# Expert activations turned by VectorE, the last two experts as half ones, sums from DRAM added by GpSimd, and the final norm in a branch

## The chip, the cores and the metric

The kernel runs on one core of a Trainium2 chip. The metric is the device time of one launch in microseconds. PE is TensorE, PEld its weight loads, DVE is VectorE, ACT is ScalarE, POOL is GpSimd, SP is SyncE, which here only issues transfers. Tensors are fp32.

## What is computed

One decoder block on 512 tokens of 1024 features. The first part (a gated linear recurrence, a dilated attention and their projections) is not touched. The second part is a mixture of 32 experts, of which each token takes four:

```python
def _clamped_swiglu(u):
    glu = jnp.minimum(u[..., ::2], SWIGLU_LIMIT)
    lin = jnp.clip(u[..., 1::2], -SWIGLU_LIMIT, SWIGLU_LIMIT)
    return glu * jax.nn.sigmoid(SWIGLU_ALPHA * glu) * (lin + 1.0)
...
    u = xb @ w_up[e] + b_up[e]            # w_up[e] 1024 x 2048
    return _clamped_swiglu(u) @ w_down[e] + b_down[e]   # w_down[e] 1024 x 1024
...
    x = x + _moe(_rmsnorm(x, norm2_g[l]), ...)
return _rmsnorm(x, final_norm_g)
```

The weights of one expert are 8 MB (up) and 4 MB (down), all 32 are 403 MB, and each is read once.

## The kernel before

**Places.** The experts are done in 32 places, numbered p. DVE ranks experts 2 to 31 by their number of tokens (`order_experts`) and sends the fuller ones to the "big" places. A big place (`BIG`) has three groups of 32 token slots, 96 slots, a half one (`LESS`) has two groups, 64 slots; `groups(p)` says which. Before, places 0 and 1 and the even ones from 4 to 30 are big, the others half, 16 of each. By the reference's routing of these inputs, the 16 big places (experts 0 and 1 and the 14 fullest others) hold 1247 tokens in 1536 slots. Slots without a token hold a dump row: numbers of 512 and above, which are rows behind the 512 real ones. What does not fit in a place would go through further blocks (`TURNS`, `CNT`), and with these inputs there are none.

**Weights.** SP loads weights in transfers of 2 MB, a "pair" of chunks of 1 MB, into a ring of nine pair buffers (18 chunks, `RAW`). An expert has four up pairs and two down pairs. `load_pair` waits on `chunk_used` until PE is done with the pair nine places back in the same buffer.

**A step.** `moe_step` of place p is on PE: the up product of p (8 chunks, L1867), then the down product of p - 1 (4 chunks, L1887). In the down product, behind its first chunk, PE turns the gathered rows of p + 1 (L1836), and behind its third the activations of p (`a_transposed`, L1844, into PSUM). Each chunk's product is made of matmuls of 32 output columns in four quarters of the array; a fp32 matmul shows as two records. ACT makes silu and the linear half from PSUM (L801, L802), DVE clips and multiplies them (L1431, L1434) and copies the turned activations out of PSUM (`a_rows`, L1425), after the down product of p - 1 has read the old ones. The product of p is then taken one step later.

**Results.** For a big place ACT and DVE write gated rows to SBUF (L828, L1472), and GpSimd adds them to rows in DRAM with an indirect transfer (`scatter`, L616), 96 rows each. For a half place ACT and DVE write the rows as two fp32r parts (`y_highs` L816, `y_lows` L1445), and PE moves them to their tokens with eight products with a 0/1 matrix (`move`, L1904), between the chunks of the next up product; DVE adds each of the eight to X in SBUF (L1459). GpSimd gathers the rows of p + 2 from DRAM (L603, L607).

**Order.** It is written by hand: two places, then places 2 to 7 written out (`PEELED`), a loop of two rounds over 12 places, and the end. The end before is: down product of place 30 (big), down product of 31 (half), eight moves into four banks, DVE's adds, then the sums in DRAM, which SP has loaded once the last scatter is through (`XF`, L568), added by DVE (L1547), and then the final norm: ACT squares (L914), DVE's small steps (L931 to L942) and scaling (L1555), and the store (L584).

## Time and profile before

| | us |
|---|---|
| median of 3 runs | 1376.93 (1376.87 to 1378.17) |
| the profiled execution, its own time | 1378.45 |
| its span, first to last instruction | 1376.6 |
| PE busy / DVE busy / ACT busy / POOL busy | 1290.3 / 525.5 / 305.8 / 76.6 |
| bytes moved | 455.28 MB, mean 331 GB/s |

The page cuts the span into 40 slices of 34.4 us. The experts start at about 320 us and the last weights land at about 1334 us. A busy PE is not one at its peak, since matmul ends are modelled. "idle before <- X" in a row says what the engine waited for; "issue" is time in which it waited for nothing that the profile shows.

### The profile page before, as it was taken

Reading aid. Unit: us, or ns where it says so; the run is one execution under the profiler, and the core shown is the slowest. Engines: PE = TensorE matmul, PEld = TensorE weight load, DVE = VectorE, ACT = ScalarE, POOL = GpSimd, SP = SyncE. Lnnn points to the kernel's source line nnn. Section 1 sums busy time; section 2 is a strip of 40 time slices with the busy share of each in tenths; the row PEclk is TensorE's granted clock in tenths of the full one; section 3 lists DMA queues with packets and bytes.
Section 4 is the critical chain, followed back from the end, with each engine's and each line's share of the span. In section 5 each row is a group of like instructions: output and inputs, shape, how many; then the busy total and the mean of one; then the engine's idle time right before and its main releaser. Section 6 shows DMA issues by size and latency. Waiting matters only on the chain.

```text
span 1376.6 us, 31492 instructions
## 1 busy us (share of the span) xinstructions
PE 1290.3 (94%) x13175; PEld 657.3 (48%) x13176; DVE 525.5 (38%) x1076; ACT 305.8 (22%) x615; POOL 76.6 (6%) x108
## 2 busy tenths in 40 slices
PE   7999989999999999999999898997999999899982
PEld 6888876685443344443434343433444444343331
DVE  5766745563223534132323222232223131323235
ACT  6454333320021112112111111111112111111112
POOL 0000001100000000000000000000000000000000
PEclk9999999999999999999999999999999999999996
DMA  9522146148999999999999999999999999999954
GB/s 294 155 67 87 47 164 264 68 172 337 328 371 400 407 401 406 399 391 398 412 398 410 399 406 405 401 411 403 399 399 411 400 411 402 407 404 405 413 229 146
DMA packets 69790, 455.28 MB, mean 331 GB/s; under 512 B 6725, under 2 KB 35557, under 8 KB 44960
## 3 DMA queue, kind: packets, MB, share of 16 engines
q1 hardware_dynamic: 64688, 438.52, 79.7%
q0 software_dynamic: 4944, 14.53, 4.3%
q8 instruction: 114, 1.87, 0.6%
q14 instruction: 44, 0.36, 0.1%
HBM read 441.91 MB, written 13.63 MB: 331 GB/s over the span
## 4 chain that ended last, share of the span: by engine, by line
PE 63%; DMA 30%; DVE 4%; issue 2%; ACT 1%; SPq 0%; DVEq 0%
PE psum L1867 24%; DMA w_raw_pair<-w_up 21%; PE psum L1887 15%; DMA w_raw_pair<-w_down 6%; PE psum L1612 5%; PE psum L1609 3%; DMA w_in_raw<-w_in 2%; PE psum L1904 2%; PE psum L1836 2%; PE psum L1698 2%; PE psum L1746 2%; PE psum L1722 1%; PE psum L1844 1%; PE psum L1685 1%; PE psum L1940 1%
## 5 line engine op out<-in xcount | busy, mean ns | idle before, releaser
L1867 PE MATMUL psum<-w_raw_pair,x_slots 128*32 128x512 f32 x5120 | 577.8, 599 | 26.8 <-DMA w_raw_pair<-w_up 25.3
L1867 PEld LDWEIGHTS psum<-w_raw_pair,x_slots 128*32 128x32 f32 x5120 | 161.3, 110 | 390.5 <-issue 344.6
L1887 PE MATMUL psum<-w_raw_pair,a_slots 128*32 128x256 f32 x5120 | 297.4, 382 | 0.3
L1887 PEld LDWEIGHTS psum<-w_raw_pair,a_slots 128*32 128x32 f32 x5120 | 160.0, 110 | 102.8 <-DMA w_raw_pair<-w_down 2.1
L801 ACT ACTIVATE lin<-psum 128x768 f32<-128x768 f32 (+1 forms) x32 | 22.5, 704 | 546.2 <-PE psum L1867 546.2
L1459 DVE TENSOR_TENSOR x_rows<-x_rows,psum 128x512 f32<-128x512 f32 x128 | 81.9, 683 | 119.3 <-PE psum L1904 119.3
L1431 DVE TENSOR_SCALAR lin<-lin 128x768 f32<-128x768 f32 (+1 forms) x32 | 15.8, 493 | 290.4 <-ACT lin L801 290.4
L1425 DVE TENSOR_SCALAR a_slots<-psum 128x768 f32<-128x768 f32 (+1 forms) x32 | 26.4, 825 | 201.0 <-PE psum L1887 199.9
L816 ACT ACTIVATE y_parts<-psum,gate_t 32x256 fp32r<-32x256 f32 x128 | 59.7, 466 | 129.7 <-PE psum L1887 128.1
L828 ACT ACTIVATE y_rows<-psum,gate_t 32x256 f32<-32x256 f32 x96 | 44.6, 465 | 188.5 <-PE psum L1887 187.5
L1445 DVE SCALAR_TENSOR_TENSOR y_parts<-psum,gate_t,y_parts 32x256 fp32r<-32x256 f32 x128 | 61.6, 481 | 29.9 <-ACT y_parts L816 28.3
L1612 PE MATMUL psum<-h_low,w_in_high 128*128 128x512 f32 x160 | 63.3, 396 | 0.0
L1612 PE MATMUL psum<-h_high,w_in_high 128*128 128x512 f32 x160 | 62.3, 389 | 0.0
L1612 PE MATMUL psum<-h_high,w_in_low 128*128 128x512 f32 x160 | 62.3, 389 | 0.0
L1904 PE MATMUL psum<-y_parts,token_sel 128*128 128x512 f32 x128 | 48.1, 462 | 6.3 <-issue 6.3
L1472 DVE TENSOR_SCALAR y_rows<-psum,gate_t 32x256 f32<-32x256 f32 x96 | 46.5, 485 | 14.3 <-issue 13.0
L1904 PEld LDWEIGHTS psum<-y_parts,token_sel 128*128 128x128 f32 x128 | 20.1, 195 | 58.7 <-issue 58.5
L1421 DVE COPY x_slots<-psum 128x768 f32<-128x768 f32 (+1 forms) x32 | 26.4, 825 | 55.2 <-PE psum L1836 43.5
L603 POOL COPY gather_rows<-row_t 96x1 int32 x32 | 5.7, 179 | 732.5 <-PE psum L1836 711.0
L1836 PEld LDWEIGHTS psum<-shape_consts,gathered 96*128 96x128 f32 (+1 forms) x256 | 33.1, 213 | 13.6 <-issue 13.6
L1836 PE MATMUL psum<-shape_consts,gathered 96*128 96x96 f32 (+1 forms) x256 | 37.9, 289 | 0.0
L977 DVE TENSOR_TENSOR w_in_low<-w_in_raw,w_in_high 128x1024 fp32r<-128x1024 f32 x24 | 29.3, 1222 | 21.5 <-ACT w_in_high L701 21.4
(285 smaller groups left out, 1108.5 us busy)
## 6 DMA issues: line engine op xcount, KB each, us to landing
w_raw_pair<-w_up SPq DMA_DIRECT2D x128, 2048.0 KB, 40.2
w_raw_pair<-w_down SPq DMA_DIRECT2D x64, 2048.0 KB, 39.7
w_in_raw<-w_in SPq DMA_DIRECT2D x28, 512.0 KB, 3.8
w_buf<-w_out SPq DMA_DIRECT2D x4, 1024.0 KB, 8.4
expert_rows<-zero_rows SPq DMA_DIRECT2D x5, 512.0 KB, 7.5
x_rows<-x SPq DMA_DIRECT2D x4, 512.0 KB, 4.8
x_rows<-x SPq DMA_DIRECT2D x1, 2048.0 KB, 17.3
normed_rows<-h_rows SPq DMA_DIRECT2D x4, 512.0 KB, 2.6
```

Of the source, the lines that this page charges most:

```text
L816: ins = act.activation(YP[quarter(g), 0, j * 256:(j + 1) * 256], Yp2[r, g, :], ACT.Copy, scale=gate_t[r, g, bass.ds(column, 1)])
L828: ins = act.activation(Y[quarter(g), j * 256:(j + 1) * 256], Yp2[r, g, :], ACT.Copy, scale=gate_t[r, g, bass.ds(column, 1)])
L977: ins = dve.tensor_tensor(WPL[:, c % 4, :, :], WPR[:, c % 2, :, :], WPH[:, c % 4, :, :].bitcast(F32), ALU.subtract)
L1445: ins = dve.scalar_tensor_tensor(low, Yp2[quarter(j), g, :], gate_t[quarter(g), g, bass.ds(column, 1)], YP[quarter(g), 0, c].bitcast(F32), ...
L1459: dve.tensor_tensor(x_part, x_part, PS[:, banks[m % len(banks)], :], ALU.add).then_inc(added, 1)
L1472: ins = dve.tensor_scalar(Y[quarter(g), j * 256:(j + 1) * 256], Yp2[r, g, :], gate_t[r, g, bass.ds(column, 1)], None, ALU.mult)
L1609: ins = pe.matmul(blocks_of(o), h_part[:, k, j * P:(j + 1) * P], w_rows, start=(k == 0 and h_part is HL), stop=(k == DK - 1 and w_part is ...
L1612: ins = pe.matmul(o, w_part[:, j, k, :], h_part[:, k, :], start=(k == 0 and h_part is HL), stop=(k == DK - 1 and w_part is WPL))
L1836: ins = pe.transpose(T[:, k, 0:rows], XG[0:rows, at_k:at_k + 2 * P - 1:2], ident[0:rows, 0:rows])
L1867: ins = pe.matmul(U[quarter(j), g, :], xs[:, c, quarter(g)], up_columns(w, j), start=False, stop=(c == UPC - 1))
L1887: ins = pe.matmul(Yp2[quarter(j), g, :], As[:, 2 * g + h, quarter(c)], raw[q.slot(m)][:, at_w:at_w + 256], start=False, stop=(c == DNC - 1 ...
L1904: ins = pe.matmul(o, SELT[:, tok], YP[:, 0, c], start=True, stop=True)
```

## The change

- **Activations.** PE's turns of the activations go. DVE turns `glu` in blocks of 32 x 32 from SBUF to SBUF (`transpose`, one instruction a place), with ALPHA folded into ACT's scales. So that this is enough, the columns of each quarter of the up product are chosen otherwise (`up_columns`), and ACT reads PSUM in steps of eight words in place of two.
- **Places.** Place 2 becomes big and place 30 half, so that the last big one is 28. Four places are written out ahead of the loop and four behind it.
- **The end.** Place 31 gets buffers and banks of its own (`As_last`, `Yp_last`, `SELT_last`). The first six moves of place 30 stand between the second and third chunk of the down product of 31, in six banks, and the moves of 31 add up on top of them in PSUM (`move_last`), so that DVE adds eight times for both. `y_highs` signals each quarter in place of each half.
- **Sums from DRAM.** SP loads them as soon as the up product of 30 is through and the last scatter has landed, and GpSimd adds them to X (L667 of the new file).
- **Scatters** get a bound of 511 beyond which a row is skipped, as the gathers have. The gathers behind place 31 are gone.
- **Norm.** DVE's last part stands in a branch taken when there are no further blocks, ahead of the code for them. The bookkeeping for such blocks is done in steps 2 and 3, not 3 to 6.

```diff
-PEELED = 8
+PEELED = 4
 BODY = 12
-ITERS = (NE - PEELED) // BODY
+ITERS = 2
+AFTER = PEELED + BODY * ITERS
...
-        XF = over("expert_sums", [P, TT, D], pair_at[0])
-        GF = over("final_g_rows", [P, D], pair_at[OVER_PAIR])
+        XF = over("expert_sums", [P, TT, D], pair_at[OVER_PAIR])
+        GF = over("final_g_rows", [P, D], pair_at[OVER_PAIR + 2])
...
-        Uflat = PS[:, 0:BIG, :].rearrange("p b (f two) -> p (b f) two", two=2)
+        Uflat = PS[:, 0:BIG, :].rearrange("p b (m f t two) -> p (b m) t f two", m=2, t=4, two=2)
...
+        Yp_last = Tflat.rearrange("p (g f) -> p g f", f=256)
...
-            return BIG if p < 2 or (p > 2 and p % 2 == 0) else LESS
+            return BIG if p < 3 or (p % 2 == 0 and p < NE - 2) else LESS
 
         def nth(p):
 
-            return {0: 0, 1: 1, 2: 0}.get(p, p // 2)
+            if groups(p) == BIG:
+                return p if p < 2 else p // 2 + 1
+            return p - (NE - HALVES) if p >= NE - 2 else (p - 3) // 2
...
+            sp.wait_ge(chunk_used, step_chunks(NE - 1).count(0))
             accv = acc_dram[0:SEQ, :].rearrange("(t p) d -> p t d", p=P)
             for i in range(TT):
...
-                                        compute_op=ALU.add).then_inc(acc_added, 16)
+                                        compute_op=ALU.add, bounds_check=SEQ - 1, oob_is_err=False).then_inc(acc_added, 16)
...
+                if ahead is not None:
+                    gather(ahead.expert, expert_at(ahead.expert), x_before, ahead.n * STEP)
...
-            scatter(Place(NE - 2))
+            for p in range(AFTER, NE - 1):
+                moe_step(Place(p - 2), Place(p + 2) if p + 2 < NE else None, use_x(p + 1))
+            pool.wait_ge(added, (MOVED - 1) * MOVES)
+            for i in range(TT):
+                pool.wait_ge(S(f"xf_in{i}"), 16)
+                pool.tensor_tensor(X[:, i, :], X[:, i, :], XF[:, i, :], ALU.add).then_inc(S("xf_added"), 1)
...
-                    act.wait_ge(a_ready, q)
-                act.activation(LN[:, 0:n * 256], Uflat[:, 0:n * 256, 1], ACT.Copy, bias=1.0).then_inc(lin_ready, 1)
-                act.activation(SG[:, 0:n * 256], Uflat[:, 0:n * 256, 0], ACT.Silu, scale=ALPHA).then_inc(u_free, 1)
+                    act.wait_ge(a_turned, q)
+                lin, sig = (b[:, 0:n * 256].rearrange("p (m t f) -> p m t f", t=4, f=STEP) for b in (LN, SG))
+                act.activation(lin, Uflat[:, 0:2 * n, :, :, 1], ACT.Copy, bias=1.0 / ALPHA, scale=1.0 / ALPHA).then_inc(lin_ready, 1)
+                act.activation(sig, Uflat[:, 0:2 * n, :, :, 0], ACT.Silu, scale=ALPHA).then_inc(u_free, 1)
...
             outputs(Place(NE - 2), END.count(0))
-            bias_row(BSD, of_place(NE - 1), bsd_ready)
-            outputs(Place(NE - 1), END.count(DNC))
+            last_column = expert_at(NE - 1)
+            act.wait_ge(acc_added, BIGS * 16)
+            act.wait_ge(chunk_used, END.count(DNC))
+            y_highs(LESS, last_column, Yp_last, 1)
...
-                act.wait_ge(S("rows_done"), i + 1)
+                act.wait_ge(added, more * MOVES + ((MOVED - 1) * MOVES + 2 * i + 2))
...
-            def a_rows(use, n):
-                dve.wait_ge(t_full, use + 1)
-                dve.tensor_scalar(As[:, 0:2 * n, :], T[:, 0:2 * n, :], 1.0 / ALPHA, None, ALU.mult).then_inc(t_free, 1)
+            def a_rows(q, n, slots):
+                dve.wait_ge(a_ready, q + 1)
+                dve.transpose(slots[:, 0:n, :, :].rearrange("p g b s -> p (g b s)"), GL[:, 0:n, :].rearrange("p g f -> p (g f)")
+                              ).then_inc(a_turned, 1)
...
-            blocks_in = {3: further_blocks, 4: block_starts, 5: block_offsets, 6: block_values}
+            blocks_in = {2: (further_blocks, block_starts), 3: (block_offsets, block_values)}
...
-            outputs(Place(NE - 2), END.count(0), LAST_BANKS)
-            token_sels(groups(NE - 1), expert_at(NE - 1))
-            outputs(Place(NE - 1), END.count(DNC), LAST_BANKS)
...
+            y_lows(HALVES - 2, LESS, expert_at(NE - 2), Yp2, 0)
+            token_sels(LESS, last_column, SELT_last)
+            y_lows(HALVES - 1, LESS, last_column, Yp_last, 1)
+            for i in range(TT):
+                dve.wait_ge(S("xf_added"), i + 1)
+                for m in (i, i + TT):
+                    dve.wait_ge(moved, (MOVED - 1) * MOVES + (m + 1))
+                    add_part(by_half(m), LAST_BANKS[m]).then_inc(added, 1)
...
+            links, rooted = link_count[0], roots[0]
+            with dve.If(nx < 1):
+                finish()
...
-            dve.wait_ge(added, HALVES * MOVES)
-            for i in range(TT):
-                dve.wait_ge(S(f"xf_in{i}"), 16)
-                dve.tensor_tensor(X[:, i, :], X[:, i, :], XF[:, i, :], ALU.add).then_inc(S("rows_done"), 1)
...
-            def a_transposed(q, use, n):
-                pe.wait_ge(a_ready, q + 1)
-                pe.wait_ge(t_free, use)
-                for g in range(n):
-                    for h in range(2):
-                        ins = pe.transpose(T[:, 2 * g + h, :], GL[:, g, h::2], ident)
-                ins.then_inc(t_full, 1)
...
-                return w.rearrange("p (k f s r) -> p k s f r", k=2, s=2, r=4)[:, j // 2, j % 2, :, :]
+                return w.rearrange("p (m j r) -> p j m r", m=2, j=4)[:, j, :, :]
...
+            def move_last(m, sel, part):
+
+                i, half = by_half(m)
+                return pe.matmul(PS[:, LAST_BANKS[m], :], sel[:, i * P:(i + 1) * P], YP[:, part, half * 512:(half + 1) * 512],
+                                 start=(part == 0), stop=(part == 1))
...
-                    if c == 2:
-                        a_transposed(p, use_a(p), n)
...
-            pe.wait_ge(u_free, NE)
-            down_bias(NE - 1, use_a(NE - 1), groups(NE - 1), (y_ready, BIGS * 2))
+            for p in range(AFTER, NE):
+                moe_step(p, step_chunks(p), Place(p - 2), groups(p - 1), groups(p), groups(p + 1) if p < NE - 1 else None)
+            down_bias(NE - 1, LESS, (t_free, OVER), Yp_last)
             for c in range(DNC):
-                down_chunk(END, c, c, groups(NE - 1))
+                if c == 2:
+                    pe.wait_ge(u_free, NE)
+                    pe.wait_ge(token_sel, HALVES - 1)
+                    pe.wait_ge(y_low, 2 * HALVES - 2)
+                    pe.wait_ge(added, (MOVED - 1) * MOVES)
+                    for m in range(6):
+                        move_last(m, SELT, 0)
+                down_chunk(END, c, c, LESS, As_last, Yp_last)
+            pe.wait_ge(token_sel, HALVES)
             for m in range(MOVES):
-                move(nth(NE - 1), groups(NE - 1), m, LAST_BANKS)
+                if m % TT == 0:
+                    pe.wait_ge(y_low, 2 * HALVES - 1 + m // TT)
+                if m >= 6:
+                    move_last(m, SELT, 0)
+                move_last(m, SELT_last, 1).then_inc(moved, 1)
```

How instructions stand on PE at the end of the expert part, before (`w_raw_pair` with a number is a pair buffer, `a_slots` the turned activations, `y_parts` and `token_sel` the two sides of a move):

```order
L1887 MATMUL psum<-w_raw_pair_112,a_slots 32x256 [waits raw_landed0]
L1887 MATMUL psum<-w_raw_pair_112,a_slots 32x256 x23
L1844 MATMUL psum<-shape_consts,glu 128x128 [waits t_free]
L1844 MATMUL psum<-shape_consts,glu 128x128 x3
L1887 MATMUL psum<-w_raw_pair_112,a_slots 32x256 x24
L1877 MATMUL psum<-bias_down_parts,bias_sel_down 32x256 [waits bsd_ready,y_ready,t_free,u_free]
L1887 MATMUL psum<-w_raw_pair_113,a_slots 32x256 [waits raw_landed1]
L1887 MATMUL psum<-w_raw_pair_113,a_slots 32x256 x31
L1887 MATMUL psum<-w_raw_pair_114,a_slots 32x256 [waits raw_landed2]
L1904 MATMUL psum<-y_parts,token_sel 128x512 [waits token_sel,y_low]
L1904 MATMUL psum<-y_parts,token_sel 128x512 x3
L1904 MATMUL psum<-y_parts,token_sel 128x512 [waits added] x4
```

And now, from the same place, the last chunks of the down product of 30, to the last move:

```order
L1930 MATMUL psum<-w_raw_pair_112,a_slots 32x256 [waits raw_landed0]
L1930 MATMUL psum<-w_raw_pair_112,a_slots 32x256 x31
L1920 MATMUL psum<-bias_down_parts,bias_sel_down 32x256 [waits t_free,bsd_ready,a_turned]
L1930 MATMUL psum<-w_raw_pair_113,a_slots_last 32x256 [waits raw_landed1]
L1930 MATMUL psum<-w_raw_pair_113,a_slots_last 32x256 x31
L1954 MATMUL psum<-y_parts,token_sel 128x512 [waits y_low,added,token_sel,u_free]
L1954 MATMUL psum<-y_parts,token_sel 128x512 x5
L1930 MATMUL psum<-w_raw_pair_114,a_slots_last 32x256 [waits raw_landed2]
L1930 MATMUL psum<-w_raw_pair_114,a_slots_last 32x256 x31
L1954 MATMUL psum<-y_parts,token_sel_last 128x512 [waits y_low,token_sel]
L1954 MATMUL psum<-y_parts,token_sel_last 128x512 [waits y_low]
L1954 MATMUL psum<-y_parts,token_sel_last 128x512
```

The turn of `glu` is gone from the down product, the wait on `y_ready` became one on `t_free` and `a_turned`, and six moves stand ahead of the last two chunks.

On DVE, from the last activations to the final part, before:

```order
L1425 TENSOR_SCALAR a_slots<-psum 128x512 [waits t_full]
L1472 TENSOR_SCALAR y_rows<-psum,gate_t 32x256
L1452 TENSOR_SCALAR token_sel<-token_numbers,row_twice 128x512
L1445 ISA [waits y_high]
L1445 SCALAR_TENSOR_TENSOR y_parts<-psum,gate_t,y_parts 32x256
L1459 TENSOR_TENSOR x_rows<-x_rows,psum 128x512 [waits moved] x8
L1528 TENSOR_LOAD counts_i [waits items_ready,blocks_known]
L1530 COMPARE_AND_BRANCH
```

And now:

```order
L1455 STREAM_TRANSPOSE a_slots_last<-glu 128x512 [waits a_ready]
L1565 TENSOR_LOAD counts_i [waits items_ready,blocks_known]
L1475 ISA [waits y_high]
L1475 SCALAR_TENSOR_TENSOR y_parts<-psum,gate_t,y_parts 32x256
L1483 TENSOR_SCALAR token_sel_last<-token_numbers,row_twice 128x512
L1475 REGISTER_ALU [waits y_high]
L1488 TENSOR_TENSOR x_rows<-x_rows,psum 128x512 [waits moved,xf_added]
L1488 TENSOR_TENSOR x_rows<-x_rows,psum 128x512 [waits moved]
L1589 COMPARE_AND_BRANCH
L960 TENSOR_SCALAR small<-small 128x2 [waits ssf,gf_in]
L1585 SCALAR_TENSOR_TENSOR final_out<-x_rows,small,final_g_rows 128x1024 [waits dve_link]
```

DVE's last activations no longer wait for PE's turn, the reading of the block count (`counts_i`) moved ahead of the last parts, and behind the eight adds there is one branch and then the norm, with no load of counts.

## Rows read from the trace of the kernel before

**Rows 1.** The page, part 2: DMA busy share in tenths, 40 slices.
```profile
DMA  9522146148999999999999999999999999999954
```

**Rows 2.** Windows: stretch, then PE, PEld, DVE, ACT, POOL busy; PEclk, DMA share, GB/s.
```profile
348.00:352.00 4.00, 3.86 (x36) 0.83 (x28) 3.72 (x15) 0.00 (x0) 0.99 (x1) 1.00 0.70 264
352.00:356.00 4.00, 3.89 (x34) 1.73 (x38) 1.01 (x2) 0.00 (x0) 0.00 (x0) 1.00 0.79 242
1200.00:1300.00 100.00, 97.82 (x1171) 41.50 (x1164) 24.62 (x42) 14.98 (x32) 7.72 (x11) 1.00 1.01 407
1333.00:1334.00 1.00, 0.28 (x8) 0.00 (x0) 0.56 (x1) 0.54 (x2) 0.00 (x0) 1.00 0.22 82
1338.00:1339.00 1.00, 1.00 (x16) 0.56 (x12) 0.00 (x0) 0.00 (x0) 0.71 (x1) 0.50 0.00 0
```

**Rows 3.** Chain that ended last: start us, us, what.
```profile
459.53 3.59 PE psum L1887 x64
...
496.74 20.60 PE psum L1867 x192
...
557.61 20.60 PE psum L1867 x192
...
670.34 2.59 PE psum L1887 x48
...
735.40 2.78 PE psum L1887 x48
```

**Rows 4.** The same chain, at the loop's second round.
```profile
944.68 6.55 issue
```

**Rows 5.** GpSimd's queue, 1021 to 1035 us, one scatter: packets, MB, share.
```profile
q0 software_dynamic: 112, 0.39, 14.1%
```

**Rows 6.** GpSimd's queue, 1320 to 1334 us, a gather of dump rows alone.
```profile
q0 software_dynamic: 80, 0.00, 0.3%
```

**Rows 7.** Timeline of PE, first steps: start us, us, instructions merged.
```profile
377.95 0.99 PE L1844 MATMUL psum<-shape_consts,glu 128*128 128x128 f32 x6
...
381.94 13.92 PE L1867 MATMUL psum<-w_raw_pair,x_slots 128*32 128x512 f32 x128
```

**Rows 8.** Timeline of PE in the last up product.
```profile
1310.88 1.92 PE L1867 MATMUL psum<-w_raw_pair,x_slots 128*32 128x512 f32 x16 [0.56 <-DMA w_raw_pair<-w_up]
...
1315.26 0.73 PE L1904 MATMUL psum<-y_parts,token_sel 128*128 128x512 f32 x2
```

**Rows 9.** Timeline of all engines, the end.
```profile
1330.48 2.80 PE L1887 MATMUL psum<-w_raw_pair,a_slots 128*32 128x256 f32 x48
...
1337.58 0.62 PE L1877 MATMUL psum<-bias_down_parts,bias_sel_down 96*32 96x256 bf16 x8 [4.30 <-DVE y_rows L1472]
...
1337.96 8.48 PE L1887 MATMUL psum<-w_raw_pair,a_slots 128*32 128x256 f32 x128
...
1346.60 3.83 ACT L816 ACTIVATE y_parts<-psum,gate_t 32x256 fp32r<-32x256 f32 x8 [9.96 <-PE psum L1887]
...
1348.64 3.95 DVE L1445 SCALAR_TENSOR_TENSOR y_parts<-psum,gate_t,y_parts 32x256 fp32r<-32x256 f32 x8 [10.69 <-ACT y_parts L816]
...
1352.70 4.20 PE L1904 MATMUL psum<-y_parts,token_sel 128*128 128x512 f32 x8 [6.26 <-issue]
1353.50 4.87 DVE L1459 TENSOR_TENSOR x_rows<-x_rows,psum 128x512 f32<-128x512 f32 x8 [0.90 <-PE psum L1904]
...
1360.94 4.63 DVE L1547 TENSOR_TENSOR x_rows<-x_rows,expert_sums 128x1024 f32<-128x1024 f32 x4 [2.57 <-issue]
...
1365.48 0.16 DVE L931 TENSOR_SCALAR small<-small 128x2 f32<-128x2 f32 x1
...
1370.31 2.48 DVE L1555 SCALAR_TENSOR_TENSOR final_out<-x_rows,small,final_g_rows 128x1024 f32<-128x1024 f32 x2
```

**Rows 10.** Line 594, GpSimd's adds of two SBUF operands: ns min/median/max.
```profile
L594 POOL TENSOR_TENSOR w_out_low<-w_buf,w_out_high x4: 2350/2356/2364, 206.0 to 250.0; 128x1024 fp32r<-128x1024 f32 x4
```

**Rows 11.** The page, part 5: DVE's copy of the turned activations.
```profile
L1425 DVE TENSOR_SCALAR a_slots<-psum 128x768 f32<-128x768 f32 (+1 forms) x32 | 26.4, 825 | 201.0 <-PE psum L1887 199.9
```

202 lines of the change are left out of this document (113 added, 89 removed).

## Prediction

> **What bounds the kernel now.** I read the DMA row of the page first: from the eleventh slice to the 38th, some 345 to 1307 us, the DMA engines are busy nine tenths or more [rows 1]. The windows say it finer: from 1200 to 1300 us the share is 1.01 at 407 GB/s, while PE has 2.2 us without work [rows 2]. So the weights set the pace in the middle. The chain of waits says how near PE is. Where PE is not short of weights, one pair of places (a big and a half one) takes 557.61 - 496.74 = 60.87 us; where it is, 735.40 - 670.34 = 65.06 us [rows 3]. Those 65.06 us are what 25.2 MB of weights and the rows of tokens cost the DMA engines. A stall of 6.55 us on PE, where the loop begins its second round, stands in the chain too [rows 4], but the ring takes it: loads go on while PE stands. In the middle, then, an edit counts only if it takes something off the DMA engines or if PE loses more than the ring holds.
>
> At the two ends it is otherwise. In the first steps the ring is full and the loads wait for PE: from 348 to 356 us the DMA share is 0.70 and 0.79 [rows 2]. At the end the last weights land at about 1334.1 us (the DMA rate is 82 GB/s in the microsecond before and then nothing) [rows 2], and behind them stand PE, ACT and DVE in turn until DVE's last scaling ends at 1370.31 + 2.48 = 1372.79 [rows 9]: 38.7 us, then 3.8 us for the last store. This tail is where most of the change's time must come from.
>
> **Scatters: 4.0 us less DMA.** In the 14 us around one scatter GpSimd's queue takes 14.1% of the engines, 1.97 us for 96 rows, 0.0205 us a row [rows 5]. A gather of nothing but dump rows takes 0.3% of 14 us, 0.04 us [rows 6]; so a skipped row is as good as free. Before, 15 scatters lie ahead of the last weights (that of place 30 comes behind): 15 x 1.97 = 29.6 us. Now all 16 do, with 1247 real rows: 1247 x 0.0205 = 25.6 us. The difference is 4.0 us. Bounds: if a scatter costs by the transfer and not by the row, the sixteenth costs 2.0 us more; if the dump rows also slow the weights beside them, 6 us less. I take 4.0.
>
> **PE's turns: nothing in the middle.** A big place loses 0.99 us of turns on PE [rows 7], some 1.7 us a pair with the half one; PE's pace goes from 60.9 to about 59 us, and DMA's stays at 65.06 less 0.4. PE only waits more. What hides the new DVE instruction: it may start once the down product of p - 1 is through, and is wanted after the up product of p + 1, 13.92 us or more later [rows 7]. The trace has no such turn; the copy that it replaces takes 825 ns [rows 11], the lower bound is nothing, and up to 13 us would be hidden. The same holds for ACT's reads in wider steps. Without that cover each microsecond would cost 32.
>
> **Place 2 big: about nothing.** A big up product is 20.60 us [rows 3], a half one 13.92 [rows 7], so in step 2, while the ring is full, PE frees its buffers 6.7 us later. Against that stand the turns gone in step 1 and in the down product of place 0, about 1 us each [rows 7]. Followed buffer by buffer: up to the down product of place 0 loads start 1 to 2 us earlier. Then PE gives back six buffers in some 33.5 us (20.6 of up product, 10.8 of down product, which is 3/2 of twice 3.59 [rows 3], and 2 of biases and turned rows), when the DMA engines, at 65.06 / 12 = 5.4 us a buffer, want 32.5. The 1 us lost there meets the 1 to 2 us won before it. I take 0, with -1.5 to +2. The bookkeeping, put into steps 2 and 3, lies on DVE behind `x_rows` and ahead of a turn that is wanted 14 us later.
>
> **The tail: 14.9 us less.** In the clock of before, weights land 4.0 us earlier, the last at 1330.1. The third pair of the last up product came at 1310.8 [rows 8] and the last pair of all at 1334.1, five pairs later (one of that product, two of each down product): 4.66 us each. So now:
> - PE goes on in the up product of 31 at 1306.9, a chunk and two moves each 2.5 us (1.92 + 0.73, overlapping [rows 8]), to 1316.2.
> - The down product of 30 is a half one, 3.59 us for two chunks [rows 3]: its last pair lands at 1320.8, it ends at 1324.5. The wait of 4.30 us on `y_rows` [rows 9] is gone, since 31 has banks of its own.
> - Its first two chunks for place 31 need the pair of 1325.5 and end at 1329.1. ACT and DVE have the parts of 30 done 5.1 us after 1324.6 (before: 1352.59 - 1346.60 = 6.0 us [rows 9], less 0.9 since DVE starts on a quarter, not on a half), at 1329.7. PE waits 0.7 us; six moves at 0.37 us take 2.2, to 1332.1. The last two chunks end at 1335.7.
> - ACT and DVE do the parts of 31: 1335.9 to 1341.1. Meanwhile PE makes four moves, behind it six more. Before, with PE idle for 6.26 us, eight moves took 4.20 us [rows 9], 0.53 to 0.6 each, at a granted clock that had been 0.50 just before [rows 2]. At that pace the last is done by 1344.9, ahead of DVE.
> - DVE's eight adds take 4.87 us [rows 9], to 1346.2.
> - DVE's adds of the sums in DRAM (4.63 us) and the 2.57 us ahead of them [rows 9] are off the path. GpSimd's adds take 2.36 us each [rows 10]: the sums, 2 MB behind the last weights, land between 1331.5 and 1336, so the fourth add ends at about 1341.5, and DVE wants it at 1345.
> - One branch, 0.4 us (an estimate between nothing and the 2.57 us that the loads and branches took before [rows 9]); then norm and scaling as before, 1372.79 - 1365.48 = 7.3 us [rows 9]: 1353.9.
>
> From the last weights to the last scaling that is 23.8 us against 38.7, 14.9 less.
>
> The Trainium skill (SBUF — State Buffer, Who interferes with whom) says that GpSimd and a VectorE instruction in a two-port mode or with two SBUF inputs hold a shared port pair in turn, the loser standing for the whole instruction. No row here shows the two side by side at such work. By that rule `token_sel_last` or an early part of the norm could stand behind one add.
>
> **Sum.** 4.0 + 0 + 0 + 14.9 = 18.9 us. The profiled execution goes from 1378.45 to 1359.5 (span 1376.6 to 1357.7); the median of the runs, 1376.93, lies 1.5 us below that execution, and goes to 1358.0.
>
> **Rivals.**
> - The tail as said, but no gain from the scatters (a transfer costs by itself, or the weights' rate doesn't rise when they shrink): 1358.0 + 4.0 to 6.0, some 1362 to 1364. For it: the packets stay at 112 and 80 where bytes go to zero [rows 5, 6]. Against: their time does not stay. 0.15.
> - A new wait in the tail: GpSimd's adds. The fourth has 3.5 us to spare. If the sums land late or an add stands behind DVE's work for its 2.36 us twice, DVE's adds wait; with all four behind DVE's parts, at 1341.1 + 9.4 = 1350.5 and two adds after, it ends at 1351.7 and not 1346.2: 1363.5. For it: four steps in series of SP, DMA, GpSimd and DVE. Against: SP may issue the loads behind the last weights, some 30 us before they land. 0.1.
> - The other side: with less to do, PE drops to half clock in the middle. It falls to 0.50 after 4.3 us without work [rows 2, 9]. Of each microsecond at half clock half is lost, and PE has 64.6 - 59 = 5.6 us to spare in a pair of places, so beyond 11.2 us at half clock in each pair PE is the bound. At 17 us that is 8.5 - 5.6 = 2.9 us a pair, 44 us over 15 pairs, less 18.9: 1402. Against it: in the stretch of 1200 to 1300 us, with 2.2 us of gaps, the clock is 1.00 [rows 2], and the new gaps are of a microsecond each. 0.03.
> - The change does little: the weights landing earlier doesn't pass on since PE stalls at the loop's exit, now ahead of place 28 (6.55 us as in [rows 4], after which only three pairs of places remain), and the tail gives only the adds and the branch, 7 us: 1370. 0.05.
>
> The Trainium skill (TensorE: Matmul & The Clock Gate, HAM oscillation) warns of the third: waits for transfers in each tile of a thin product bring the clock down each time. The trace so far does not agree for gaps of this size, with 1.00 in that window.
>
> **How the numbers follow.** My forecast has 0.67, its own range 1354 to 1362 (scatters -2, start -1.5, tail -1 on one side; start +2, half clock in the last chunks +2 on the other). The second and third cases reach to 1364, the last beyond. The range of 1353.5 to 1366 leaves out the 0.08 of the last two and a little of each side. 0.2% is 2.8 us, which a measurement of this kernel can tell from none. Faster 0.95, same 0.02, slower 0.03.
>
> **What would show it.** In the profile after: the last weight lands 4 us earlier; GpSimd's queue about 1.6 us a scatter; PE idles more before w_up and w_down pairs, with the clock near 1; no down product waits on the DVE turn; the end is as timed above, last scaling at about 1354. It is wrong if the weights land no earlier, if PE or DVE waits for GpSimd's adds, if the clock is below 0.9 in the middle, or if the DMA share is below 0.9 after 390 us.

## The result and the profile after

The changed kernel takes 1365.36 us (median of 4 runs, 1363.16 to 1367.53), the one before, timed beside it, 1377.33 (1376.87 to 1378.17). The ratio is 0.9914, with a 95% interval of 0.9900 to 0.9929. That is 12.0 us faster: inside the range, but 18.9 had been forecast. The profiled execution is the quickest of the four, 1363.16 us with a span of 1361.3, so the traces differ by more than the medians: 1376.6 - 1361.3 = 15.3 us. Of these, 2.0 lie ahead of the experts (their first up product starts at 317.90 and not 319.89), where nothing was changed. In the fourteen traces of this study that start lies anywhere between 316.45 and 320.57.

The page after, part 2, the DMA row to [rows 1]; and of part 5 PE's up product and DVE's turn:

```profile
DMA  9523137148999999999999999999999999999982
...
L1910 PE MATMUL psum<-w_raw_pair,x_slots 128*32 128x512 f32 x5120 | 583.8, 604 | 48.2 <-DMA w_raw_pair<-w_up 48.1
...
L1455 DVE STREAM_TRANSPOSE a_slots<-glu 128x768 f32<-128x768 f32 (+1 forms) x31 | 26.3, 850 | 164.4 <-PE psum L1930 164.4
```

The engines are as full as before, PE waits 48.1 us for up weights (25.3 before), and DVE's turn takes 850 ns where the copy out of PSUM took 825 [rows 11]. No matmul waits for it. The windows that answer to [rows 2]:

```profile
348.00:352.00 4.00, 4.00 (x44) 1.15 (x40) 2.91 (x7) 0.00 (x0) 0.00 (x0) 1.00 0.68 168
352.00:356.00 4.00, 4.00 (x40) 1.08 (x36) 0.00 (x0) 0.00 (x0) 0.00 (x0) 1.00 0.93 377
1200.00:1300.00 100.00, 89.63 (x1072) 36.15 (x1064) 27.49 (x49) 18.35 (x41) 5.41 (x7) 1.00 1.01 410
1333.00:1334.00 1.00, 1.00 (x10) 0.51 (x11) 0.00 (x0) 0.00 (x0) 0.02 (x1) 1.00 0.15 61
1338.00:1339.00 1.00, 0.00 (x0) 0.00 (x0) 0.31 (x1) 0.96 (x3) 1.00 (x2) 1.00 0.00 0
```

From 1200 to 1300 us PE now has 10.4 us without work, where it had 2.2, and the granted clock stays at 1.00, the higher level of 2.4 GHz. That window is a good one: from 560 to 1280 us the mean is 0.98 (0.99 before), and from 700 to 800 us, where PE has 9.4 us without work, it is 0.95. GpSimd's queue from 1010 to 1024 us, around one scatter, to [rows 5]:

```profile
q0 software_dynamic: 114, 0.32, 11.6%
```

So a scatter costs the engines 0.116 x 14 = 1.62 us on the mean, where it was 1.97. That is what was forecast; and yet the weights land hardly earlier, as the next section shows. The stall at the loop's second round, to [rows 4], in the chain:

```profile
811.73 5.58 issue
```

The end, timeline of all engines, to [rows 8, 9]:

```profile
1315.83 0.73 PE L1948 MATMUL psum<-y_parts,token_sel 128*128 128x512 f32 x2
...
1318.46 3.64 PE L1930 MATMUL psum<-w_raw_pair,a_slots 128*32 128x256 f32 x64
...
1322.52 3.66 PE L1930 MATMUL psum<-w_raw_pair,a_slots 128*32 128x256 f32 x64 [0.42 <-DMA w_raw_pair<-w_down]
...
1327.39 3.66 PE L1930 MATMUL psum<-w_raw_pair,a_slots_last 128*32 128x256 f32 x64 [0.99 <-DMA w_raw_pair<-w_down]
1327.96 3.98 DVE L1475 SCALAR_TENSOR_TENSOR y_parts<-psum,gate_t,y_parts 32x256 fp32r<-32x256 f32 x8 [6.87 <-ACT y_parts L833]
...
1332.20 1.62 PE L1954 MATMUL psum<-y_parts,token_sel 128*128 128x512 f32 x6 [1.15 <-DVE y_parts L1475]
...
1333.75 3.66 PE L1930 MATMUL psum<-w_raw_pair,a_slots_last 128*32 128x256 f32 x64
1333.98 9.30 POOL L667 TENSOR_TENSOR x_rows<-x_rows,expert_sums 128x1024 f32<-128x1024 f32 x4 [61.30 <-DMA expert_sums<-expert_rows]
1337.63 3.86 ACT L833 ACTIVATE y_parts<-psum,gate_t 32x256 fp32r<-32x256 f32 x8 [6.89 <-PE psum L1930]
1338.69 3.97 DVE L1475 SCALAR_TENSOR_TENSOR y_parts<-psum,gate_t,y_parts 32x256 fp32r<-32x256 f32 x8 [6.23 <-ACT y_parts L833]
...
1340.79 1.34 PE L1954 MATMUL psum<-y_parts,token_sel_last 128*128 128x512 f32 x4 [3.38 <-DVE y_parts L1475]
...
1343.55 4.27 DVE L1488 TENSOR_TENSOR x_rows<-x_rows,psum 128x512 f32<-128x512 f32 x7 [0.17 <-PE psum L1954]
...
1344.50 0.35 SPq L595 DMA_DIRECT2D final_g_rows<-final_norm_g  x1
...
1348.87 0.17 DVE L960 TENSOR_SCALAR small<-small 128x2 f32<-128x2 f32 x1 [1.04 <-DMA final_g_rows<-final_norm_g]
...
1351.40 5.18 SPq L599 DMA_DIRECT2D out<-final_out  x4
...
1353.71 2.48 DVE L1585 SCALAR_TENSOR_TENSOR final_out<-x_rows,small,final_g_rows 128x1024 f32<-128x1024 f32 x2
```

These rows show the order that the change wanted: PE goes from the down product of place 30 into that of 31, six moves stand in the middle of it, GpSimd adds the sums beside all this, and DVE has nothing but its eight adds between its last part and the norm. One wait is new. The end of the chain that ended last says what is behind it:

```profile
1333.98 3.57 POOL x_rows L667 x2
1338.31 2.65 POOLq L113
1340.96 2.33 POOL x_rows L667
1344.50 4.34 DMA final_g_rows<-final_norm_g
1350.09 2.48 DVE final_out L1585 x2
```

SP issues the load of the final gains only after GpSimd's fourth add, and DVE waits 1.04 us for it.

**When the weights are there.** A pair of weights raises its semaphore sixteen times. The trace has the time of each, and for the last pair of all (the second down pair of place 31) these are, in us of the span:

```
before       1306.3 1318.7 1319.4 1320.4 1320.9 1324.5 1324.7 1325.7 1326.9 1330.1 1330.8 1332.3 1333.5 1334.4 1335.0 1335.2
after        1299.2 1300.4 1306.7 1313.9 1314.7 1317.0 1318.2 1320.7 1320.7 1321.9 1323.0 1327.0 1327.4 1327.8 1331.2 1332.2
```

I read them as one by each DMA engine. The Trainium skill (DMA: Bandwidth & Descriptors, Why a DMA increments its semaphore by 16 and not by 1) says just this, and that only the full count means that all has landed. The engines are some 30 us apart, and PE can start only when the last of them is through. They drift apart during the stream: in the trace of after the pair issued at 388.4 us lands from 396.7 to 398.9, the one issued at 689.5 from 707.6 to 731.7, and the one issued at 1018.6 from 1026.9 to 1060.4. With that, the last weights of before are there at 1335.2 (I had 1334.1 from the windows), and after at 1332.2. Counted from the experts' start it is 1015.3 and 1014.3 us: in this pair of traces the middle gained 1.0 us and not 4. Even that can't be told from nothing. The traces of kernels with the loads of before have 1013.1 to 1015.3 us there (`before`, `b_skip`, `b_turn`), and those with the loads of after 1012.8 to 1015.2 (`after`, `after_again`, `a_noskip`, `a_gf_early`, `g_dve_sums`, `g_norm_last`; the next section has the kernels). From the last landing to the end of the last scaling it is 1372.79 - 1335.2 = 37.6 us before and 1356.19 - 1332.2 = 24.0 after, 13.6 less, of 14.9 forecast. The store behind it ends 5.1 us later where it was 3.8. 2.0 + 1.0 + 13.6 - 1.3 = 15.3.

### The profile page after: what moved, and what is told of

Its sections match the earlier page's. It is cut to its first block, busy times and chain, and to the rows that moved or that the text cites. A ratio compares the mean times of both kernels' runs of the same rounds, so it can differ in the third digit from the quotient of the medians.

```text
span 1361.3 us, 31013 instructions
## 1 busy us (share of the span) xinstructions
PE 1261.3 (93%) x13007; PEld 633.7 (47%) x13008; DVE 515.7 (38%) x1064; ACT 305.8 (22%) x615; POOL 83.2 (6%) x108
## 4 chain that ended last, share of the span: by engine, by line
PE 57%; DMA 37%; DVE 3%; ACT 1%; issue 1%; POOL 0%; POOLq 0%; SPq 0%; DVEq 0%; ACTq 0%
DMA w_raw_pair<-w_up 25%; PE psum L1910 22%; PE psum L1930 12%; DMA w_raw_pair<-w_down 6%; PE psum L1663 5%; PE psum L1660 3%; DMA expert_sums<-expert_rows 3%; PE psum L1948 2%; DMA w_in_raw<-w_in 2%; PE psum L1749 2%; PE psum L1887 2%; PE psum L1797 2%; PE psum L1773 1%; PE psum L1736 1%; PE psum L1985 1%
## 5 line engine op out<-in xcount | busy, mean ns | idle before, releaser
L1910 PE MATMUL psum<-w_raw_pair,x_slots 128*32 128x512 f32 x5120 | 583.8, 604 | 48.2 <-DMA w_raw_pair<-w_up 48.1
L1930 PE MATMUL psum<-w_raw_pair,a_slots 128*32 128x256 f32 x4992 | 281.8, 380 | 1.4 <-DMA w_raw_pair<-w_down 1.3
L1488 DVE TENSOR_TENSOR x_rows<-x_rows,psum 128x512 f32<-128x512 f32 x120 | 76.9, 683 | 132.2 <-PE psum L1948 132.0
L1455 DVE STREAM_TRANSPOSE a_slots<-glu 128x768 f32<-128x768 f32 (+1 forms) x31 | 26.3, 850 | 164.4 <-PE psum L1930 164.4
L1451 DVE COPY x_slots<-psum 128x512 f32<-128x512 f32 (+1 forms) x31 | 25.4, 820 | 54.7 <-PE psum L1887 43.0
L1948 PE MATMUL psum<-y_parts,token_sel 128*128 128x512 f32 x112 | 41.1, 448 | 0.0
L1948 PEld LDWEIGHTS psum<-y_parts,token_sel 128*128 128x128 f32 x112 | 16.6, 188 | 47.2 <-issue 47.2
L1887 PEld LDWEIGHTS psum<-shape_consts,gathered 64*128 64x128 f32 (+1 forms) x248 | 32.1, 214 | 13.2 <-issue 13.2
L1887 PE MATMUL psum<-shape_consts,gathered 64*128 64x64 f32 (+1 forms) x248 | 36.7, 289 | 0.0
```

Source lines behind the costliest of these rows:

```text
L1488: return dve.tensor_tensor(x_part, x_part, PS[:, bank, :], ALU.add)
L1887: ins = pe.transpose(T[:, k, 0:rows], XG[0:rows, at_k:at_k + 2 * P - 1:2], ident[0:rows, 0:rows])
L1910: ins = pe.matmul(U[quarter(j), g, :], xs[:, c, quarter(g)], up_columns(w, j), start=False, stop=(c == UPC - 1))
L1930: ins = pe.matmul(banks[quarter(j), g, :], slots[:, g, 2 * c + h, :], raw[q.slot(m)][:, at_w:at_w + 256], start=False, stop=(c == DNC - 1 ...
L1948: ins = pe.matmul(o, SELT[:, tok], YP[:, 0, c], start=True, stop=True)
```

## The experiments

Every kernel was timed beside the kernel before, in four groups. Its medians there were 1377.25 us (with `after_again`, `a_noskip`, `a_gf_early` and `b_skip`), 1376.21 (`a_sc32_skip`, `a_sc32_rows`, `a_sc_none`, `b_turn`), 1377.87 (`a_sc32_even`, `g_dve_sums`, `g_norm_last`) and 1376.21 (`a_spread`). In brackets stands the ratio to the kernel before with its 95% interval. Between groups the ratios are the better comparison.

**The result again, the bound alone, and an earlier load.** `after_again` is the changed kernel with no edit. `a_noskip` is it without the bound on the scatters, `b_skip` the kernel before with that bound:

```diff
-                                        compute_op=ALU.add, bounds_check=SEQ - 1, oob_is_err=False).then_inc(acc_added, 16)
+                                        compute_op=ALU.add).then_inc(acc_added, 16)
```

`a_gf_early` is the changed kernel with the final gains loaded ahead of SP's wait for GpSimd's adds, when there are no further blocks:

```diff
+            with sp.If(nx < 1):
+                sp.wait_ge(chunk_used, NC * NE - UPC + 2)
+                sp.dma_start(GF[:, :], final_g...).then_inc(S("gf_in"), 16)
...
-            sp.wait_ge(chunk_used, more * NC + (NC * NE - UPC + 2))
-            sp.dma_start(GF[:, :], final_g...).then_inc(S("gf_in"), 16)
+            with sp.If(nx > 0):
+                sp.wait_ge(chunk_used, more * NC + (NC * NE - UPC + 2))
+                sp.dma_start(GF[:, :], final_g...).then_inc(S("gf_in"), 16)
```

after_again:

> The changed kernel itself once more, for its spread and as the neighbour of the runs beside it. Its four times so far go from 1363.2 to 1367.5 us where those of before go from 1376.9 to 1378.2. Expected: a median of 1364 to 1366, 11 to 13 us under before; the last weight pair lands at about 1332 us of the span, some 3 us ahead of before, and the last adds end near 1348.

a_noskip:

> The changed kernel without the bound on the scatters: all 96 rows are added again. Theory M (the prediction's: the 16 DMA engines share the rows, so the weights gain the mean time of a skipped row): 289 rows x 0.0205 us = 5.9 us slower than the changed kernel. Theory S (each weight pair lands when the slowest of 16 engines is through, and the skipped rows lie on others): 0 to 1.5 us slower, the last landing of the pairs unchanged.

b_skip:

> The kernel before with nothing changed but the bound on the scatters. Theory M: 15 scatters ahead of the last weights with 18 rows less each, 0.0205 us a row: 5.5 us faster than before. Theory S: 0 to 1.5 us faster.

a_gf_early:

> The changed kernel with the final gains loaded, in the usual case, ahead of SyncE's wait for GpSimd's adds and not behind it. In the changed kernel DVE's first step of the norm waits 1.04 us for that load, which was issued at 1344.5. Expected if that wait ends last: about 1.0 us faster. Rival, that the load of 512 KB then stands in the queues ahead of the sums from DRAM or beside the last weights and costs as much: no change.

Measured: `after_again` 1363.72 us (ratio 0.9905, 0.9888 to 0.9922), so the gain is 12.0 to 13.5 us. `a_noskip` 1362.87 (0.9895, 0.9878 to 0.9912) and `b_skip` 1376.94 (0.9996, 0.9986 to 1.0006): no gain by the bound shows in either kernel. 5.9 and 5.5 us had been expected if the mean over the engines were the price of a skipped row, and both lie outside the intervals, so that price falls. `a_gf_early` 1362.38 (0.9890, 0.9872 to 0.9909) is 1.3 us under `after_again`, which is what the wait is in the traces (1.38 us in that of `after_again`), though the two intervals overlap. DVE's first step of the norm there stands right behind the adds:

```profile
1344.68 4.28 DVE L1492 TENSOR_TENSOR x_rows<-x_rows,psum 128x512 f32<-128x512 f32 x7 [0.17 <-PE psum L1958]
1348.87 0.16 DVE L964 TENSOR_SCALAR small<-small 128x2 f32<-128x2 f32 x1
```

**What a scatter costs.** Three kernels from the changed one. In `a_sc32_skip` rows 32 to 95 of every scatter are sent out of bounds, in `a_sc32_rows` the scatter has 32 rows, in `a_sc_none` there is none. What is not scattered is missing from the output.

```diff
# a_sc32_skip
+            pool.memset(IDXS[:, :], 600).then_inc(idxs_ready, 1)
...
-                pool.tensor_copy(IDXS[0:BLK, 0:1], row_t[0:BLK, ...
+                pool.tensor_copy(IDXS[0:STEP, 0:1], row_t[0:STEP, ...
# a_sc32_rows
-   pool.indirect_dma_start(acc_dram, ...(IDXS[0:BLK, 0:1], 0), Y[0:BLK, :], None,
+   pool.indirect_dma_start(acc_dram, ...(IDXS[0:STEP, 0:1], 0), Y[0:STEP, :], None,
# a_sc_none
-   pool.indirect_dma_start(acc_dram, ...).then_inc(acc_added, 16)
+   pool.sem_inc(acc_added, 16)
```

a_sc32_skip:

> The changed kernel, but each scatter adds only its first 32 slots: the numbers of slots 32 to 95 lie beyond the bound and are skipped (so two thirds of the big places' rows are left out of the result). It still has 96 descriptors. Theory M (the engines' mean counts): 16 scatters lose about 46 real rows each of 78, 16 x 46 x 0.0205 = 15 us faster than the changed kernel. Theory S (each engine has six slots in a row, and the first ones keep all their work): no change, 0 to 2 us. Theory F (a scatter costs by its descriptors, real or not): no change either.

a_sc32_rows:

> The same 32 slots added, but by a scatter of 32 descriptors (the same rows are left out). Its work is the same as that of a_sc32_skip. Theory M: as a_sc32_skip, 15 us faster than the changed kernel. Theory S: the 32 rows are dealt out anew, two to each of 16 engines in place of six, so the slowest engine loses four rows of 0.33 us: 16 x 1.3 = 21 us faster, until PE at 59 us a pair of places bounds it. Theory F: two thirds of 16 x 1.97, 21 us faster too. So the pair tells M (both) from S and F (this one alone).

a_sc_none:

> The changed kernel with no scatter at all, only its semaphore (the big places' rows are left out of the result). The whole worth of the scatters: 16 x 1.97 = 31 us by the mean, somewhat more if the slowest engine has more than its share. It is the scale for the two beside it.

Measured: 1360.55, 1345.10 and 1336.25 us (0.9889, 0.9770, 0.9714). `a_sc32_skip` is 3.2 us under `after_again` by the medians and 2.2 by the ratios, where 15 had been expected by the mean and 0 to 2 by theory S. The other two gained 18.6 and 27.5 us by the medians, of 21 and 31 expected. The first two carry the same 32 rows and differ by 15.4 us. Two explanations were left. Either a skipped row costs as much as a carried one (theory F). Or each of the 16 engines has six rows in a run, 0 to 5, 6 to 11 and so on, so that skipping rows 32 to 95 leaves the first five engines with six full rows, and the fullest engine sets the pace (theory S). `a_sc32_even` tells them apart: all 96 rows, 64 of them out of bounds, but rows 0, 1, 6, 7, 12, 13 and so on are the ones carried.

```diff
-    cols["dump_row"] = np.concatenate([SEQ + p, 0 * p], 1)
+    cols["dump_row"] = np.concatenate([SEQ + p, SEQ + p + 2048 * (p % 6 >= 2)], 1)
...
+                dve.tensor_scalar(row_x[0:BLK, 0:NE], rows[:, 0:NE, 0], cst("dump_row")[0:BLK, 1:2], None, ALU.add)
...
-                pool.tensor_copy(IDXS[0:BLK, 0:1], row_t[0:BLK, ...
+                pool.tensor_copy(IDXS[0:BLK, 0:1], row_x[0:BLK, ...
...
-                            compute_op=ALU.add, bounds_check=SEQ - 1, ...
+                            compute_op=ALU.add, bounds_check=SEQ + P - 1, ...
```

> The changed kernel with 96 descriptors a scatter of which 64 are skipped by the bound, as in the run with rows 32 to 95 skipped, but the 32 that are carried stand at rows 0, 1, 6, 7, 12, 13 and so on, not at 0 to 31 (most real rows of tokens are left out, so the output is not the reference's). Theory S, that each of the 16 DMA engines has six rows in a run and the engine with six full ones sets the pace: now each has two full rows, so the time should be that of the scatter with 32 descriptors, about 1345 us (1343 to 1349). Theory F, that a descriptor costs the same whether it is carried or skipped: as the run with rows 32 to 95 skipped, 1360 to 1363 us.

Measured: 1342.76 us (0.9748, 0.9726 to 0.9769). Theory F falls. GpSimd's queue from 560 to 1280 us, in `a_sc32_skip`, and then in `a_sc32_even`:

```profile
q0 software_dynamic: 3421, 7.04, 3.5%
```

```profile
q0 software_dynamic: 3424, 7.04, 3.5%
```

The same packets (within three), bytes and share, and 17.8 us between them (19.4 by the ratios). From the experts' start to the last landing it is 1012.1 us in `a_sc32_skip` and 994.6 in `a_sc32_even`, which is where `a_sc32_rows` stands too (994.1). Only which engine has the rows differs, and the sixteen landings of the last pair show it:

```
a_sc32_skip  1301.3 1301.3 1301.4 1301.4 1301.7 1302.0 1302.5 1303.5 1303.7 1306.0 1314.7 1318.5 1321.9 1324.2 1324.3 1330.6
a_sc32_even  1282.0 1294.3 1295.2 1296.0 1296.7 1298.9 1300.5 1300.7 1302.2 1303.2 1305.4 1305.4 1307.0 1307.8 1311.7 1311.9
```

With rows 0 to 31 real, ten engines are through within 5 us of each other, and six come up to 25 us later: 32 rows in sixes fill five engines and a third of a sixth. The Trainium skill (DMA: Bandwidth & Descriptors, Why a DMA increments its semaphore by 16 and not by 1) says that a transfer takes the most engines, up to 16, that divide the slowest dimension of both its sides, and names a 96-partition tile as one for 16; that makes six rows an engine. That they are neighbours fits these landings; the trace does not name the engine of a row.

The price follows: from `after_again` to `a_sc32_even` an engine with full rows has four rows less in each of 16 scatters, (1363.7 - 1342.8) / 64 = 0.33 us a row (0.34 by the ratios, 0.28 by the traces from the experts' start to the last landing). [rows 5] had it all along: 0.141 x 14 us x 16 engines / 96 rows = 0.33 us. I had divided it by 16.

**The activations' turn alone.** `b_turn` is the kernel before with DVE's turn and nothing else of the change.

```diff
-    act.activation(LN[:, 0:n * 256], Uflat[:, 0:n * 256, 1], ACT.Copy, bias=1.0).then_inc(lin_ready, 1)
+    act.activation(lin, Uflat[:, 0:2 * n, :, :, 1], ACT.Copy, bias=1.0 / ALPHA, scale=1.0 / ALPHA).then_inc(lin_ready, 1)
...
-                dve.tensor_scalar(As[:, 0:2 * n, :], T[:, 0:2 * n, :], 1.0 / ALPHA, None, ALU.mult).then_inc(t_free, 1)
+                dve.transpose(As[:, 0:n, :, :]..., GL[:, 0:n, :]...).then_inc(a_turned, 1)
...
-                    if c == 2:
-                        a_transposed(p, use_a(p), n)
```

> The kernel before with the first part of the change alone: activations turned by DVE, the up product's columns and ACT's reads changed with it, everything else as before. Forecast: nothing in the middle, since the weights set the pace there, and up to 1.5 us faster from the start and the turn gone ahead of the last chunks (0.74 us of PE). If an unseen cost of the turn or of the wider reads lay on the path, it would be slower.

Measured: 1373.82 us (0.9983, 0.9971 to 0.9995), 2.4 us faster than before, with an interval of 0.7 to 4.0. Its trace has 1013.1 us from the experts' start to the last landing (before 1015.3, `b_skip` 1013.9) and 36.2 from there to the last scaling (before 37.6, `b_skip` 37.4). So of the 2.4 us, 1.2 to 1.4 lie in the tail. What is known to be gone there is the turn of place 31 on PE, a half place, ahead of the last chunk of place 30; in the trace of before:

```profile
1329.81 0.74 PE L1844 MATMUL psum<-shape_consts,glu 128*128 128x128 f32 x4
```

The rest is of the size by which such traces differ from each other.

**The tail's other two parts.** Both start from `a_gf_early`. In `g_dve_sums` DVE adds the sums from DRAM behind its eight adds, in `g_norm_last` the norm stands behind the code for further blocks. The reading of the block count stays where the changed kernel has it, ahead of the last parts, although the expectation below has VectorE read it behind its adds.

```diff
# g_dve_sums
-            for i in range(TT):
-                pool.wait_ge(S(f"xf_in{i}"), 16)
-                pool.tensor_tensor(X[:, i, :], X[:, i, :], XF[:, i, :], ALU.add)...
...
+            for i in range(TT):
+                dve.wait_ge(S(f"xf_in{i}"), 16)
+                dve.tensor_tensor(X[:, i, :], X[:, i, :], XF[:, i, :], ALU.add)...
# g_norm_last
-            with dve.If(nx < 1):
-                finish()
...
-            with dve.If(nx > 0):
-                finish()
+            finish()
```

g_dve_sums:

> The kernel with the final gains loaded early (1362.4 us), but the sums in DRAM are added by VectorE after its eight adds, as in the kernel before, instead of by GpSimd. If the prediction's step is right (GpSimd's adds took VectorE's 4.63 us off the path), this costs 4 to 5 us: 1366.4 to 1367.4. Rival: VectorE's own adds were stretched by GpSimd working beside it, or VectorE waited for GpSimd; then the cost is 0 to 2 us: 1362.4 to 1364.4.

g_norm_last:

> The kernel with the final gains loaded early (1362.4 us), but the norm stands behind the code for further blocks, as in the kernel before, so VectorE reads the count and passes the branches ahead of it. If the prediction's step is right (2.57 us before, 0.4 us now), this costs 1.5 to 2.5 us: 1363.9 to 1364.9. Rival: the time of the branches is hidden behind the waits for the last moves either way: below 0.5 us.

Measured: `g_dve_sums` 1366.64 us (0.9920, 0.9903 to 0.9938), 4.3 more than `a_gf_early`; by ratios it is 0.9920 - 0.9890, 4.1 us, give or take some 3.5, and the traces agree: from the last landing to the last scaling it is 27.8 us against 22.8. The row that does it, in its timeline:

```profile
1341.12 4.28 DVE L1489 TENSOR_TENSOR x_rows<-x_rows,psum 128x512 f32<-128x512 f32 x7 [0.17 <-PE psum L1959]
1345.42 4.63 DVE L1578 TENSOR_TENSOR x_rows<-x_rows,expert_sums 128x1024 f32<-128x1024 f32 x4
```

DVE's own seven adds take 4.28 us there and 4.27 where GpSimd had been adding just before: nothing was stretched. `g_norm_last` 1365.10 (0.9909, 0.9891 to 0.9928), 2.7 more than `a_gf_early`, and by the two intervals that can be nothing. Its trace shows only 0.42 us between the adds and the norm:

```profile
1346.65 4.28 DVE L1492 TENSOR_TENSOR x_rows<-x_rows,psum 128x512 f32<-128x512 f32 x7 [0.17 <-PE psum L1953]
1351.35 0.17 DVE L964 TENSOR_SCALAR small<-small 128x2 f32<-128x2 f32 x1 [0.42 <-issue]
```

From the last landing to the last scaling it has 1358.68 - 1335.3 = 23.4 us, against 22.8 in `a_gf_early`. So passing the branches costs about 0.5 us, close to the rival's value, and some 2 of the 2.7 are not in this tail. Its experts start 0.5 us later and its weights take 1.5 us longer, for which I have no cause; the six traces of kernels with these loads differ by up to 2.4 us there.

**A version that beats both.** If the fullest engine sets the pace, the tokens of an expert should not fill its slots from the first one up. `a_spread` is `a_gf_early` with the q-th token of a big place put into slot 6 (q mod 16) + q div 16 (in a half place 4 (q mod 16) + q div 16), which gives each engine a token before any gets a second. Only the numbers from which the rows are made change; experts 0 and 1, which are set up earlier, stay as they are.

```diff
# turn_values, pos: the token's number q within its expert
+                dve.tensor_scalar(s_row, cut_row[:, :], -2.0, 6.0, ALU.mult, ALU.add)
+                dve.tensor_scalar(b_row, cut_row[:, :], 32.0, -95.0, ALU.mult, ALU.add)
+                link(dve.tensor_scalar(last_k, cut_row[:, :], -2.0, 5.0, ALU.mult, ALU.add))
...
+                link(dve.tensor_scalar(full_k, pos, 16.0, None, ALU.is_ge))
+                for k in range(2, 6):
+                    link(dve.scalar_tensor_tensor(full_k, pos, 16.0 * k, full_k, ALU.is_ge, ALU.add))
+                link(dve.tensor_tensor(lgv(3), lgv(3), row_of[2], ALU.min))
+                dve.tensor_tensor(lgv(7), lgv(7), row_of[0], ALU.mult)
+                link(dve.tensor_tensor(lgv(3), lgv(3), row_of[1], ALU.mult))
+                link(dve.tensor_tensor(pos, pos, full_k, ALU.add))
+                link(dve.tensor_tensor(lgv(6), spread(cst("tok"), NE), lgv(7), ALU.subtract))
```

> The kernel with the final gains loaded early (1362.4 us), and the tokens of each expert from the third on are given slots in turn, one for each run of six (or, in a half place, four) slots, so that the 16 DMA engines get equal numbers of real rows in scatters and gathers; 15 short VectorE instructions more, some 4 us where VectorE waits 11.6 us. From the run with evenly spread 32 rows a row on the slowest engine costs (1363.7 - 1342.8) / (16 x 4) = 0.33 us. Over the 14 scatters concerned an engine with full runs now moves 84 rows; spread, the first engine has 77 and the last 63. Theory S: 7 to 21 rows less, 2.3 to 6.9 us, and gathers, 12 to 31 rows less, at a price between nothing and the scatter's: 1 to 5 us; together 1351 to 1360 us, most likely about 1357. Rival: the weights' last landing is set by something else once the rows are even, or only skipped rows in sixes matter: 1361 to 1363.

Measured: 1355.44 us (median of 5, 1355.25 to 1357.24; 0.9844, 0.9822 to 0.9865), 6.9 us under `a_gf_early` (6.3 by the ratios) and 20.8 under the kernel before. GpSimd's queue from 560 to 1280 us, after and then spread:

```profile
q0 software_dynamic: 3396, 9.22, 5.0%
```

```profile
q0 software_dynamic: 3424, 9.28, 5.0%
```

The same load again. Its last weights land at 1325.9, 1007.1 us after the experts' start, against 1013.8 in `a_gf_early`: 6.6 us, as much as the whole gain. The run deals out scatters and gathers at once, so it doesn't say what each of them gave.

## Why the prediction held in its direction and missed a third of the gain

- **What bounds the kernel: right, and not sharp enough.** The DMA engines set the pace in the middle, but "the DMA engines" are sixteen, and a share of 1.01 over all of them hides that one pair lands on them over some 30 us. The slowest one is the bound. One sign of being wrong that the prediction names, weights that land no earlier, came as near as these traces can tell.
- **The range: in part luck.** The time lies above my own forecast's range of 1354 to 1362. It is inside 1353.5 to 1366 because that was drawn wide enough for the rivals, and the first rival is what came.
- **Scatters, 4.0 us: wrong, no gain measured.** The step that failed is "0.0205 us a row", a mean over 16 engines, and with it "a skipped row is as good as free". Tokens fill the slots from 0 up, so the bound frees the engines with the last slots, while ten engines keep six full rows in every big place with 60 tokens or more. For those a scatter costs 6 x 0.33 = 1.97 us as before, and the sixteenth scatter, which now lies ahead of the last weights, should add its 1.97 whole. The bound of my own sum "if a scatter costs by the transfer and not by the row, the sixteenth costs 2.0 us more" has that size, for another reason. `a_noskip` and `b_skip` show no gain by skipping; `a_sc32_even` and `a_spread` show the mechanism. That the sixteenth scatter costs 2.0 us follows from the price and was not run by itself; the times from the experts' start to the last landing, which overlap before and after, don't show it.
- **PE's turns, 0 in the middle: right within what can be told.** The turn alone gave 2.4 us, 1.2 to 1.4 of them in the tail. The DVE turn, 0.85 us, is hidden; no down product waits for it.
- **Place 2 big, 0:** not run alone. The share of DMA is 0.68 and 0.93 from 348 to 356 us, where it was 0.70 and 0.79 [rows 2], and the time from the experts' start to the last landing is the same within what traces can tell. So no cost of it shows, and no gain.
- **The tail, 14.9 us: right, 13.6 measured.** Taken from the last landing of the weights, which came 2.1 us later than forecast, each of these steps is within 0.6 us of its forecast time: last chunks done at 1337.4 (1337.8), last part 1342.7 (1343.2), adds done 1347.8 (1348.3), last scaling 1356.2 (1356.0). PE waits 1.15 us for the parts of 30 (0.7 forecast). The last landing is the mark to count from and not itself the wait that ends last: the last two chunks start at 1333.75, 1.5 us behind it, when the six moves are through. The fourth add of GpSimd ends at 1343.3 (1341.5 forecast, 1343.6 with the same shift), before DVE comes to its last two adds. Each of GpSimd's adds takes 2.34 to 2.37 us, as in [rows 10]. `token_sel_last` had run at 1331.97, before the first of them, so the collision that the prediction names for it did not arise here. Of the 1.3 us missed, 1.1 is my time for the last weights of before, 1334.1 by the windows and 1335.2 by the landings, taken the other way: the tail of before was 37.6 and not 38.7. Two parts were sized by experiment: the adds on GpSimd are worth 4.3 us (4.63 forecast), and the branch by itself about 0.5. I had put 0.4 where the kernel before had 2.57. In `g_norm_last`, with the norm as far back as before, that gap is 0.42, so the other 2 us are not the branch's. The count of blocks, now read ahead of the last parts, is what is left to explain them; it was not run by itself.
- **Not foreseen:** the final gains, queued on SP behind GpSimd's adds: 1.04 us in this trace, 1.3 by `a_gf_early`. The rival on GpSimd's adds named SP in its chain but looked only for a wait of DVE's adds.
- **The rivals.** The first one, no gain from the scatters, 1362 to 1364, is what came: 1363.7 in the one set of runs, and 1365.4, a little above it, in the other. I had given it 0.15 since the packets' time fell with the bytes; it did fall, and by the experiments on engines that were not the last. PE at half clock in the middle did not come: the mean granted clock is 0.98 from 560 to 1280 us, and 0.97 to 1.00 from 1200 to 1300 us in all traces here. The stall at the loop's second round is 5.58 us, and the middle did not grow by it.

In the profiled pair the sum is then 13.6 (tail) + 1.0 (middle) + 2.0 (start) - 1.3 (store). The start is not the change's: it varies by 4 us between traces. The end of the store (3.8 and 5.1 us behind the last scaling) varies by 1.7: it is 3.8 to 4.2 us in the three traces of kernels with the old end and 4.3 to 5.5 in those with the new one. Whether the new end has a part in that is open.

## What to carry to other kernels

A DMA share near 1.00 over 16 engines is a mean. Where a small indirect transfer rides beside a stream of weights, price it on the engine that has most of its rows, and deal real and skipped rows out so that each engine has as many; that gave 6 to 7 us here for 15 short instructions. Skipping rows helps only where it empties the fullest engine. And in a tail that is cut short, look at each transfer that is queued behind a wait on the same issuing engine, however small: it may be the next to be late.

## What the runs showed of the hardware

- The sixteen landings of one 2 MB pair are spread over 27 to 33 us at the end of the stream, with a ring of nine pairs between load and use, even with no scatters at all (1274.6 to 1305.8). So scatters alone don't make the spread. The gathers are still there, and whether the engines would drift apart without them was not run; which engine is slowest the trace doesn't name.
- The 96-row scatter behaves as if its rows stood in sixteen runs of six neighbours, one run an engine (`a_sc32_skip` against `a_sc32_even`), and a carried row of 4 KB added to DRAM costs its engine 0.33 us, by the queue's share and by the time of the whole kernel alike. From two rows an engine to none it was less: (1342.8 - 1336.3) / 32 = 0.20 us a row from `a_sc32_even` and (1345.1 - 1336.3) / 32 = 0.28 from `a_sc32_rows`, and 0.24 and 0.23 by the traces from the experts' start to the last landing.
- DVE's turn of 128 x 768 fp32 in blocks of 32 x 32, SBUF to SBUF, takes 0.98 us, and of 128 x 512 0.71.
